# Hybrid recurrent decoder step: score products of the odd layer issued over four quarters of the array

## The chip, the cores and the metric

One core of a Trainium2 chip runs the whole program. The engines are TensorE (PE in the profile; PEld is its weight load), VectorE (DVE), ScalarE (ACT), GpSimd (POOL) and SyncE (SP). Each has its own queue, in order, and they meet at semaphores. The metric is the device time of one execution in microseconds; lower is better.

## What is computed

A trunk of two layers is run on 512 prompt tokens and on 8 sample sequences of 4 tokens. Layer 0 mixes with GLA and HGRN2, layer 1 with RWKV-7. Each layer then has a SwiGLU and a gated input embedding. Only the RWKV-7 recurrence of layer 1 matters here, 16 heads of 64:

```
def step(s, inp):
    r_t, lw_t, k_t, v_t, kk_t, a_t = inp
    s_kk = jnp.einsum('bhik,bhk->bhi', s, kk_t)
    s = (s * jnp.exp(lw_t)[:, :, None, :]
         - s_kk[..., :, None] * (kk_t * a_t)[..., None, :]
         + v_t[..., :, None] * k_t[..., None, :])
    return s, jnp.einsum('bhij,bhj->bhi', s, r_t)
```

## The kernel before, in words

The prompt is cut into 16 chunks of 32 tokens, and the recurrence is done chunk by chunk in matrix form. The sample tokens are a seventeenth chunk. The heads stand in 8 tiles i, two heads g = 0, 1 in each (partitions 0 to 63 and 64 to 127). Four chunks make a quad; quads 0 to 3 are the prompt, quad 4 is the sample. PSUM has 8 banks: banks 0 and 1 (`ps[:, bank, :]`) belong to the preparation of a quad, banks 2 to 7 to the chunks' own chain.

**Preparation of a quad** is a list of parts, made by `parts_of` (L1779). Part number k writes bank k % 2. TensorE issues the products of each part (`pe_prepare`, L1805), one named engine then takes the bank to SBUF (`act_prepare` L1860, `dve_prepare` L1886), and the next part on that bank first waits for it (`read_by`). The parts of a prompt quad, in order:

- four score parts "sc" (L1820), one for each pair of chunks cp and head half g. Each has 16 products of 64 by 64 by 64 in fp32 (8 tiles i, two chunks par). par picks the output partitions, so the column half of the array; g picks the operands' partitions, so its row half. Each leaves two matmul records. VectorE multiplies the bank by a mask (L1905). After the last it runs a chain: four copies L1915, L1920, L1923, and `next_level` (transpose L1949, mask L1950)
- two parts "vt" of value transposes (L1825), the first copied by ScalarE with four operations (L1868), the second by VectorE with four (L1928)
- for levels 2 to 5 of a triangular inversion, a P part (L1834, copied by ScalarE L1879; it needs the mask of L1950) and an X part (L1839; VectorE subtracts it in L1933 and makes the next mask), 64 products of 32 by 32 each over four diagonal tiles, with four key transposes "kt" (L1829, copied by ScalarE L1876) between them.

That makes 18 parts. The last two preparations also hold four state parts "st" each (L1845), which transpose states that a DMA on the GpSimd queue has brought (L2075, `pool_states`); the load for b + 2 is issued after st b. Quad 4 has one chunk pair, one chunk of it, two score parts, level 2 only, and a last part "rts" with 128 small products (256 records, L1854).

**The chunks** of a quad (`pe_chunk`, L1958) are a chain: products av (L1969), products with the state R (L1986), output products with the state (L1994), slot of two parts, U (L2001), slot of one part, state products H (L2011), output products o (L2016), slot of two parts. Before U, ScalarE and VectorE copy R (L2027, L2046), before H they copy U (L2031, L2051), and VectorE updates the state after H (L2060, L2064). In the slots `go_on` takes the next parts of the preparation of quad q + 1 on each of the three engines, at the same place in each queue. So the chunks of a quad offer 20 slots. What is left of the list stands behind the last chunk (`all_quads`). The preparation of quad 0 has nothing beside it.

```
            go_on(preparation, 2)
            pe.wait_ge(*O2.act.at(f"R{n}"))
            pe.wait_ge(*O2.dve.at(f"R{n}"))
```

Of the kernel before, what the change touches and what calls it, by code (L numbers as in the profile page):

```python
# [18 lines left out]
ALU = mybir.AluOpType  # L19
# [4 lines left out]
KT = D // P  # L24
# [104 lines left out]
def trunk(nc, a, o, known, seen, stop=99):  # L129
    ctx = ExitStack()  # L130
    with ctx:
# [31 lines left out]
        ps = ctx.enter_context(nc.psum_tensor("ps", [P, 8, 512], F32))  # L163
# [62 lines left out]
        for name in order:  # L226
            used[name] = tuple(ab)
            n, units = stages[name]
# [1117 lines left out]
        O2 = Section("odd_quads")  # L1346
# [3 lines left out]
        kb = mix[:, 0:8704].rearrange("p (i n s t) -> p i n s t", i=KT, n=NCO, s=2)  # L1350
# [386 lines left out]
        QUADS = TP // P  # L1737
# [35 lines left out]
        read_by = {}  # L1773
# [5 lines left out]
        def parts_of(q):  # L1779

            ncp = quad_shape(q)[2]
            parts = [("sc", (cp, g), "dve") for cp in range(ncp) for g in range(2)]
            parts += [("vt", 0, "act"), ("vt", 1, "dve")]
# [13 lines left out]
        def part_name(q, kind, x):  # L1797
            return {"sc": lambda: f"sc{q}{x[0]}{x[1]}", "st": lambda: f"st{x}", "rts": lambda: "rts"}.get(
                kind, lambda: f"{kind}{q}{x}")()

        def taken(by, q, kind, x):

            return (O2.act if by == "act" else O2.dve).at(part_name(q, kind, x))

        def pe_prepare(pe, q):  # L1805
# [5 lines left out]
            for kind, x, by, bank in parts_of(q):  # L1811
                if bank in read_by:
                    pe.wait_ge(*read_by[bank]())
                out = ps[:, bank, :]
                if kind == "sc":
                    cp, g = x
                    for i in range(KT):
                        for par in range(min(2, len(js))):
                            n = 4 * q + 2 * cp + par
                            mm = pe.matmul(out[64 * par:64 * par + 64, i * 64:(i + 1) * 64],  # L1820
                                           kb[64 * g:64 * g + 64, i, n, :, :], qr[64 * g:64 * g + 64, i, n, :, :],
                                           start=True, stop=True)
# [34 lines left out]
                read_by[bank] = lambda by=by, q=q, kind=kind, x=x: taken(by, q, kind, x)  # L1857
# [28 lines left out]
        def dve_prepare(dve, q):  # L1886
# [13 lines left out]
            for kind, x, by, bank in parts_of(q):  # L1900
                if by == "dve":
                    name = part_name(q, kind, x)
                    dve.wait_ge(*O2.pe.at(name))
                    if kind == "sc":
                        dve.tensor_tensor(scs[q % 2][0:pr, x[0], x[1], :, :],  # L1905
                                          ps[0:pr, bank, :].rearrange("p (i t) -> p i t", i=KT),
                                          scm[0:pr, q // QUADS, :].unsqueeze(1).to_broadcast([pr, KT, 64]),
                                          ALU.mult).then_inc(*O2.dve.done(name))
                        if x == (ncp - 1, 1):
# [507 lines left out]
```

## Time and profile before

| | us |
|---|---|
| median of 3 runs | 2425.63 |
| lowest and highest | 2424.89, 2429.2 |
| profiled execution | 2422.3 |
| its span, first to last instruction | 2420.5 |
| TensorE busy | 2082.6 (86%) |
| VectorE busy | 1023.9 (42%) |
| ScalarE busy | 743.4 (31%) |
| GpSimd busy | 145.3 (6%) |

The profile is of one execution, so durations are to be held against its own time of 2422.3 us. The stage of the change lies between 1373 and 1718 us of the span. A row of the timeline gives start, duration, engine, line, operation, output and input tiles, shapes and how many instructions it merges; in brackets stands the idle time of the engine before it and what ended it. "issue" is idle time for which the profile shows nothing waited for. PEclk is the clock that TensorE was granted, as a share of 2.4 GHz.

### The profile page before, as it was taken

To read this page: it belongs to the slowest core of one execution; us is meant where nothing else is said; L and a number is where in the kernel's file an instruction comes from. 1 tells how busy PE (TensorE), PEld (TensorE's weight loads), DVE (VectorE), ACT (ScalarE), POOL (GpSimd) and SP (SyncE) were. 2 spreads that over 40 slices of the span, in tenths; PEclk is the share of its full clock that TensorE was granted. 3 is DMA by queue.
4 is the path that set the end of the run, shared out by engine and by line. 5 is a ranking of instruction groups with operands and counts; after the bars stand their busy time and mean duration, and the time that the engine had idled before them with its cause. 6 is when DMAs were issued, how large, how long until landed. Compare 5 with 4: busy or idle time off the path is not lost.

```text
span 2420.5 us, 48144 instructions
## 1 busy us (share of the span) xinstructions
PE 2082.6 (86%) x21161; PEld 1931.0 (80%) x21161; DVE 1023.9 (42%) x1401; ACT 743.4 (31%) x932; POOL 145.3 (6%) x159
## 2 busy tenths in 40 slices
PE   4997658978899999986898889889768799999987
PEld 4897547848799999984787778778447799999976
DVE  5326583134433333355578533332434433333353
ACT  3125221043443222232355111121054444122233
POOL 1000352110100000010000000000010100000010
PEclk8998655558899999998899865655567899999988
DMA  3232002011223223221121200000020223222311
GB/s 102 64 90 57 27 1 53 7 52 56 93 87 101 65 87 100 74 61 46 40 74 54 62 4 3 4 12 19 11 40 27 88 87 100 74 79 87 100 48 54
DMA packets 237101, 138.59 MB, mean 57 GB/s; under 512 B 6560, under 2 KB 232160, under 8 KB 236944
## 3 DMA queue, kind: packets, MB, share of 16 engines
q1 hardware_dynamic: 226528, 114.31, 16.4%
q0 software_dynamic: 4048, 13.67, 2.3%
q10 hardware_dynamic: 6368, 8.22, 1.1%
q8 instruction: 135, 2.21, 0.4%
q14 instruction: 22, 0.18, 0.0%
HBM read 128.02 MB, written 8.16 MB: 56 GB/s over the span
## 4 chain that ended last, share of the span: by engine, by line
PE 75%; DVE 14%; ACT 5%; issue 3%; POOL 1%; DMA 1%; ACTq 0%; DVEq 0%; POOLq 0%
PE ps L299 51%; DVE mix L496 1%; DVE x_split L516 1%; PE ps L1839 1%; PE ps L1820 1%; PE ps L1969 1%; PE ps L1986 1%; PE ps L945 1%; PE ps L1994 1%; PE ps L2011 1%; PE ps L916 1%; PE ps L906 1%; PE ps L1834 1%; PE ps L2016 1%; PE ps L2001 1%
## 5 line engine op out<-in xcount | busy, mean ns | idle before, releaser
L299 PE MATMUL ps<-x_split,w_head 128*128 128x272 f32 x5568 | 952.1, 294 | 82.6 <-DVE x_split L516 39.7
L299 PEld LDWEIGHTS ps<-x_split,w_head 128*128 128x128 f32 x5568 | 807.5, 193 | 105.0 <-issue 80.3
L299 PE MATMUL ps<-x_split,w_rest 128*128 128x272 f32 x2784 | 586.4, 293 | 0.0
L267 ACT ACTIVATE w_head<-w_raw 128x1024 fp32r<-128x1024 f32 (+1 forms) x206 | 228.8, 1111 | 799.4 <-PE ps L299 791.8
L272 DVE TENSOR_TENSOR w_rest<-w_raw,w_head 128x1024 fp32r<-128x1024 f32 (+1 forms) x206 | 265.2, 1288 | 430.5 <-ACT w_head L267 430.3
L299 PEld LDWEIGHTS ps<-x_split,w_rest 128*128 128x128 f32 x2784 | 445.5, 193 | 0.0
L299 PE MATMUL ps<-hidden_split,w_head 128*128 128x272 f32 x1408 | 233.1, 287 | 0.0
L299 PEld LDWEIGHTS ps<-hidden_split,w_head 128*128 128x128 f32 x1408 | 198.0, 188 | 0.0
L299 PE MATMUL ps<-hidden_split,w_rest 128*128 128x272 f32 x704 | 145.2, 287 | 0.0
L1125 DVE TENSOR_TENSOR hT<-hT,ps 128x544 f32 (+1 forms) x48 | 34.6, 722 | 208.2 <-PE ps L299 208.2
L299 PEld LDWEIGHTS ps<-hidden_split,w_rest 128*128 128x128 f32 x704 | 110.0, 188 | 0.0
L496 POOL TENSOR_TENSOR mix<-hT,mix 128x544 f32<-128x544 f32 x20 | 36.8, 1842 | 1097.9 <-ACT mix L480 1077.6
L866 PE MATMUL ps<-mix 64*64 64x64 f32 (+1 forms) x896 | 57.8, 314 | 47.8 <-DVE mix L774 30.4
L866 PEld LDWEIGHTS ps<-mix 64*64 64x64 f32 (+1 forms) x896 | 49.7, 217 | 53.8 <-DVE mix L774 35.4
L1241 DVE TENSOR_TENSOR mix<-mix,ps 128x544 f32<-128x544 f32 x44 | 31.8, 722 | 132.2 <-PE ps L299 132.2
L267 ACT ACT_TABLE_LOAD x21 | 26.9, 1283 | 94.5 <-PE ps L299 83.8
L843 ACT ACTIVATE mix<-mix 128x512 f32<-128x512 f32 (+1 forms) x36 | 23.0, 640 | 81.6 <-POOL mix L747 81.5
L1834 PE MATMUL ps<-odd_quad 32*32 32x32 f32 x2080 | 30.3, 228 | 18.3 <-DVE odd_quad L1950 15.2
L1834 PEld LDWEIGHTS ps<-odd_quad 32*32 32x32 f32 x2080 | 28.2, 142 | 22.3 <-issue 18.3
L746 POOL TENSOR_TENSOR mix<-mix 128x256 f32<-128x256 f32 (+1 forms) x36 | 25.9, 720 | 261.0 <-DVE mix L701 197.6
L496 DVE TENSOR_TENSOR mix<-hT,mix 128x544 f32<-128x544 f32 x20 | 30.1, 1525 | 26.0 <-ACT mix L480 25.7
L466 DVE TENSOR_TENSOR mix<-mix 128x544 f32<-128x544 f32 x48 | 34.6, 720 | 11.2 <-ACT mix L460 11.2
(353 smaller groups left out, 2459.1 us busy)
## 6 DMA issues: line engine op xcount, KB each, us to landing
w_raw<-in_w_ffn_gate SPq DMA_DIRECT2D x44, 512.0 KB, 3.9
w_raw<-in_w_ffn_up SPq DMA_DIRECT2D x44, 512.0 KB, 3.8
w_raw<-in_w_ffn_down SPq DMA_DIRECT2D x32, 704.0 KB, 4.4
w_raw<-in_w_in_even SPq DMA_DIRECT2D x29, 512.0 KB, 3.8
w_raw<-in_w_ple_gate SPq DMA_DIRECT2D x16, 512.0 KB, 3.6
w_raw<-in_w_out_even SPq DMA_DIRECT2D x8, 512.0 KB, 3.7
w_raw<-in_rw_wr SPq DMA_DIRECT2D x8, 512.0 KB, 3.6
w_raw<-in_rw_wk SPq DMA_DIRECT2D x8, 512.0 KB, 3.7
```

The source lines that it names most:

```text
L267: act.activation(wh[:, s, 0:kt * P], raw[:, s, 0:kt * P], ACT.Copy).then_inc(head_ok[s], 1)
L272: dve.tensor_tensor(wl[:, s, 0:kt * P], raw[:, s, 0:kt * P], wh[:, s, 0:kt * P].bitcast(F32), ALU.subtract).then_inc(rest_ok[s], 1)
L299: mm = pe.matmul(ps[:, 2 * s + h, 0:TH], w[:, s, k * P:(k + 1) * P], x[:, k, h * TH:(h + 1) * TH], start=first and k == 0, stop=k == kt - ...
L466: dve.tensor_tensor(n.sum, n.sum, n.sq[:, s, :], ALU.add).then_inc(sum_ok, 1)
L496: eng.tensor_tensor(n.y[:, k % 3, :], hT[:, k, :], n.rs, ALU.mult).then_inc(*signal.done(f"y{k}"))
L516: dve.scalar_tensor_tensor(out=xl[:, k, :], in0=n.y[:, k % 3, :], scalar=n.gain(k), in1=xh[:, k, :].bitcast(F32), op0=ALU.mult, op1=ALU.su ...
L746: pool.tensor_tensor(e[:, :, 0, :], mid, b[:, :, 0, :], ALU.subtract)
L866: mm = pe.matmul(ps[64 * (c % 2):64 * (c % 2) + CE, b0 + level // 2, at:at + CE], left[:, c * CE:(c + 1) * CE], right[:, c * CE:(c + 1) * CE],
L906: mm = pe.matmul(ps[:, b0, h * CE:(h + 1) * CE], vtok[r:r + CE, tt, h * DV:(h + 1) * DV], pT[r:r + CE, h, tt, :], start=h == 0, stop=c == ...
L1125: dve.tensor_tensor(h, h, out2(s), ALU.add).then_inc(bank_free[s], 1)
L1241: dve.tensor_tensor(two(prod), two(act_out), out2(1), ALU.mult).then_inc(prod_ok, 1)
L1834: mm = pe.matmul(at_block(out, tile, cp, i), at_block(bT, tile, cp, i), at_block(xx, tile, cp, i), start=True, stop=True)
```

## The change

`parts_of` now lists one score part for each chunk pair, and the value transposes stand between and behind them: sc 0, vt 0, sc 1, vt 1 (with one chunk pair: sc 0, vt 0, vt 1). A score part writes both banks, head half g into bank g, and waits until both are free. Its products run over i, then par, then g, so four neighbours take the four quarters of the array. VectorE multiplies the two banks one after the other, and both banks count as taken when the second is done. A prompt quad has 16 parts in place of 18, the sample's one less. The products, their sizes and their number stay the same.

```
--- before.py
+++ after.py
@@ -1779,8 +1779,10 @@
         def parts_of(q):
 
             ncp = quad_shape(q)[2]
-            parts = [("sc", (cp, g), "dve") for cp in range(ncp) for g in range(2)]
-            parts += [("vt", 0, "act"), ("vt", 1, "dve")]
+            parts = [("sc", 0, "dve"), ("vt", 0, "act")]
+            if ncp > 1:
+                parts += [("sc", 1, "dve")]
+            parts += [("vt", 1, "dve")]
             keys = [("kt", j, "act") for j in range(2 * ncp)]
             for level in range(2, level_count(q) + 1):
                 parts.append(("P", level, "act"))
@@ -1795,7 +1797,7 @@
             return [(kind, x, by, k % 2) for k, (kind, x, by) in enumerate(parts)]
 
         def part_name(q, kind, x):
-            return {"sc": lambda: f"sc{q}{x[0]}{x[1]}", "st": lambda: f"st{x}", "rts": lambda: "rts"}.get(
+            return {"sc": lambda: f"sc{q}{x}1", "st": lambda: f"st{x}", "rts": lambda: "rts"}.get(
                 kind, lambda: f"{kind}{q}{x}")()
 
         def taken(by, q, kind, x):
@@ -1809,17 +1811,19 @@
                     pe.wait_ge(bank_free[s], used["rw_o"][s])
                 pe.wait_ge(*O1.dve.at("nrm"))
             for kind, x, by, bank in parts_of(q):
-                if bank in read_by:
-                    pe.wait_ge(*read_by[bank]())
+                banks = (0, 1) if kind == "sc" else (bank,)
+                for b in banks:
+                    if b in read_by:
+                        pe.wait_ge(*read_by[b]())
                 out = ps[:, bank, :]
                 if kind == "sc":
-                    cp, g = x
                     for i in range(KT):
                         for par in range(min(2, len(js))):
-                            n = 4 * q + 2 * cp + par
-                            mm = pe.matmul(out[64 * par:64 * par + 64, i * 64:(i + 1) * 64],
-                                           kb[64 * g:64 * g + 64, i, n, :, :], qr[64 * g:64 * g + 64, i, n, :, :],
-                                           start=True, stop=True)
+                            n = 4 * q + 2 * x + par
+                            for g in range(2):
+                                mm = pe.matmul(ps[64 * par:64 * par + 64, g, i * 64:(i + 1) * 64],
+                                               kb[64 * g:64 * g + 64, i, n, :, :], qr[64 * g:64 * g + 64, i, n, :, :],
+                                               start=True, stop=True)
                 elif kind == "vt":
                     for i in range(4):
                         mm = pe.transpose(out[0:nt, i * P:(i + 1) * P], vF[:, 4 * x + i, q * P:q * P + nt], ident[:, :])
@@ -1854,7 +1858,8 @@
                                 mm = pe.matmul(o2[:, :, b * ST:(b + 1) * ST], hs[r, i, b, :],
                                                qr[r, i, NCO - 1, :, b * ST:(b + 1) * ST], start=True, stop=True)
                 mm.then_inc(*O2.pe.done(part_name(q, kind, x)))
-                read_by[bank] = lambda by=by, q=q, kind=kind, x=x: taken(by, q, kind, x)
+                for b in banks:
+                    read_by[b] = lambda by=by, q=q, kind=kind, x=x: taken(by, q, kind, x)
                 yield
 
         def act_prepare(act, q):
@@ -1902,11 +1907,12 @@
                     name = part_name(q, kind, x)
                     dve.wait_ge(*O2.pe.at(name))
                     if kind == "sc":
-                        dve.tensor_tensor(scs[q % 2][0:pr, x[0], x[1], :, :],
-                                          ps[0:pr, bank, :].rearrange("p (i t) -> p i t", i=KT),
-                                          scm[0:pr, q // QUADS, :].unsqueeze(1).to_broadcast([pr, KT, 64]),
-                                          ALU.mult).then_inc(*O2.dve.done(name))
-                        if x == (ncp - 1, 1):
+                        for g in range(2):
+                            dve.tensor_tensor(scs[q % 2][0:pr, x, g, :, :],
+                                              ps[0:pr, g, :].rearrange("p (i t) -> p i t", i=KT),
+                                              scm[0:pr, q // QUADS, :].unsqueeze(1).to_broadcast([pr, KT, 64]),
+                                              ALU.mult).then_inc(*O2.dve.done(f"sc{q}{x}{g}"))
+                        if x == ncp - 1:
                             dve.wait_ge(*O2.dve.at(name))
 
                             for par in range(min(2, len(js))):
```

## Rows read from the trace of the kernel before

**Rows 1.** The page, busy time of TensorE and its share of the span.
```profile
PE 2082.6 (86%) x21161; PEld 1931.0 (80%) x21161; DVE 1023.9 (42%) x1401; ACT 743.4 (31%) x932; POOL 145.3 (6%) x159
```

**Rows 2.** Windows of the stage: length, busy us, PEclk, DMA share, GB/s.
```profile
1373.59:1413.39 39.80, 26.13 (x1177) 23.29 (x1178) 16.83 (x29) 7.12 (x12) 0.00 (x0) 0.59 0.05 10
1413.39:1483.44 70.05, 62.97 (x1880) 58.17 (x1880) 26.72 (x41) 13.02 (x23) 0.00 (x0) 0.57 0.02 4
1483.44:1554.51 71.07, 62.06 (x1946) 57.46 (x1944) 27.42 (x42) 13.35 (x24) 0.00 (x0) 0.64 0.01 3
1554.51:1635.52 81.01, 69.84 (x1977) 64.34 (x1977) 28.11 (x43) 14.98 (x27) 2.46 (x3) 0.56 0.04 10
1635.52:1717.50 81.98, 78.35 (x1328) 72.61 (x1328) 21.06 (x34) 10.77 (x20) 3.54 (x5) 0.50 0.09 22
```

**Rows 3.** TensorE's waits, 1373 to 1718: total us, times, longest us.
```profile
PE ps L1834 <- DVE odd_quad L1950: 15.2, 7, 3.5
PE ps L1839 <- issue: 9.3, 11, 1.9
PE ps L1845 <- DMA mix<-in_state_rwkv: 4.3, 2, 3.9
```

**Rows 4.** Timeline, TensorE: start, us, engine line, tile, shapes, records [idle before].
```profile
1373.59 6.15 PE L1820 MATMUL ps<-mix 64*64 64x64 f32 x128 [3.06 <-DVE mix L1716]
...
1448.87 1.92 PE L1994 MATMUL ps<-mix 64*64 64x32 f32 x32
...
1450.71 1.93 PE L1834 MATMUL ps<-odd_quad 32*32 32x32 f32 x128
...
1641.17 3.28 PE L1820 MATMUL ps<-mix 64*64 64x64 f32 x32
```

**Rows 5.** Chain of work, first chunk of quad 1, 1489 to 1502.
```profile
1489.28 3.11 PE ps L1820 x61
...
1501.91 1.09 PE ps L1969 x17
```

**Rows 6.** Timeline of quad 2's preparation, VectorE and ScalarE, 1501 to 1506.
```profile
1501.64 1.72 DVE L1915 COPY odd_quad<-odd_quad 32x512 f32<-32x512 f32 x4
...
1501.94 2.43 ACT L1868 ACTIVATE odd_quad<-ps 32x512 f32<-32x512 f32 x4 [2.02 <-PE ps L1825]
1503.39 0.69 DVE L1920 TENSOR_TENSOR odd_quad<-odd_quad,tables 128x512 f32<-128x512 f32 x1
...
1504.84 0.71 DVE L1949 STREAM_TRANSPOSE odd_quad<-odd_quad 128x512 f32<-128x512 f32 x1
1505.48 0.65 DVE L1950 TENSOR_TENSOR odd_quad<-odd_quad,tables 128x512 f32<-128x512 f32 x1
```

**Rows 7.** Chain of work, a chunk with an empty slot, 1702 to 1704.
```profile
1702.94 0.71 DVE mix L2051
...
1703.78 1.97 PE ps L2011 x32
```

**Rows 8.** Timeline, TensorE, quad 3 and the sample's preparation, 1633 to 1678.
```profile
1633.11 1.08 PE L1845 MATMUL ps<-ident,mix 64*128 64x64 f32 x8 [3.94 <-DMA mix<-in_state_rwkv]
...
1648.33 1.97 PE L2011 MATMUL ps<-mix 64*64 64x64 f32 x32 [1.07 <-DVE mix L2051]
...
1678.01 13.71 PE L1854 MATMUL ps<-mix 64*64 64x8 f32 x253
```

**Rows 9.** Timeline, VectorE, last mask multiply of quad 0, 1379.8.
```profile
1379.78 0.69 DVE L1905 TENSOR_TENSOR odd_quad<-ps,tables 128x512 f32<-128x512 f32 x1 [0.66 <-PE ps L1820]
```

**Rows 10.** Windows, columns as in rows 2: two stretches at either clock.
```profile
1488.00:1504.00 16.00, 15.84 (x288) 14.89 (x287) 7.28 (x13) 3.02 (x7) 0.00 (x0) 0.50 0.01 2
1511.50:1525.20 13.70, 10.70 (x461) 9.46 (x459) 4.83 (x8) 3.70 (x7) 0.00 (x0) 1.00 0.02 5
```

**Rows 11.** Timeline, TensorE: a fifth level, and L1994 at the upper clock.
```profile
1474.16 1.87 PE L1834 MATMUL ps<-odd_quad 32*32 32x32 f32 x123 [2.22 <-DVE odd_quad L1950]
...
1519.79 1.12 PE L1994 MATMUL ps<-mix 64*64 64x32 f32 x32
```

## Prediction

> **What bounds the kernel now.** I read the page first: TensorE is busy for 2082.6 us, 86% of the span [rows 1]. The change works in one stage only, the recurrence of the odd layer, from 1373.6 to 1717.5 us. The table of windows [rows 2] shows its parts: the preparation of quad 0 alone (39.8 us), quads 0, 1 and 2 (70.0, 71.1 and 81.0 us, each with the preparation of the next quad threaded through it) and quad 3 with the sample chunk (82.0 us). In all but the first TensorE is busy 86 to 96% of the time, VectorE a quarter to two fifths, ScalarE less. So TensorE's queue sets the end, and what counts is its work plus the moments at which the next instruction in it must wait. Those waits are listed in [rows 3]. The largest are VectorE's masks before the products of L1834 (15.2 us, half of it in the preparation of quad 0, and 2.2 us before each fifth level, as [rows 11]), 4.3 us for the sample states' DMA, and stretches of "issue", where no wait is shown (9.3 us in the largest row).
>
> TensorE's clock was at its lower level (1.2 GHz) for most of the stage: means of 0.50 to 0.64 [rows 2]. I sum at that level.
>
> **What a score product costs.** One fp32 product is two matmul records. In the old order neighbours lie in the same row half of the array and in its two column halves. 128 records took 6.15 us, 48 ns each [rows 4]; in the quads 61 took 3.11 us, 51 ns each [rows 5], so a part of 32 costs 1.6 us. For the sample there is only one chunk, so all products of a part take the same quarter: 32 records in 3.28 us, about 100 ns each. So two column halves run at once and a quarter that repeats does not [rows 4]. Nothing in this trace uses four quarters of 64 by 64. The nearest rows bound it. L1834 cycles over four 32 by 32 tiles that differ in rows and columns: 128 records in 1.9 us, 15 ns each against 32 columns twice, so four at once do run. L1994 takes two diagonal quarters: 32 records in some 1.85 us before L1834 follows, 58 ns, two at once over the row halves [rows 4]. By the first the new order takes half of the old time, about 27 ns a record, 1.75 us for a pair of parts (64 records) instead of 3.2; by the second alone it would not gain, 3.25 us. I take the first, since rows and columns each split in the trace and the 15 ns row shows that the queue can feed four. What neither shows is two row halves writing the same partitions, in two banks.
>
> The Trainium skill (TensorE: Matmul & The Clock Gate, Part 3, packing small matmuls) gives sixteen tiles of rows and columns at once a measured 10.6 times, with row tiles in different banks. By that page four quarters run at once; no run here shows it yet. TensorEngine Tiling (Array Packing), PSUM Bottleneck, of the Trainium skill speaks against the change: once tiling has sped up the products, emptying PSUM may be the bound.
>
> **The change on TensorE's queue.** Before, four score parts alternate between banks 0 and 1, so the products of one run while VectorE multiplies the other by the mask. After, one part fills both banks, VectorE needs two operations of 0.69 us for it, and the next part on TensorE waits for the second of them. Queued behind that wait is everything on TensorE, the chunk's own chain too. The number of parts falls from 18 to 16 for a prompt quad, so each later part also moves to an earlier slot (two, one and two slots in each chunk).
>
> 1. *First chunk of quads 0, 1 and 2*, worked out on quad 1 [rows 5, 6]. Before, from the end of the products with the state at 1489.28 to the next chunk at 1501.91, TensorE has no gap over 0.3 us. After: scores 1.75; wait for both multiplies, 2 x 0.69 and two hand-overs of 0.1, 1.6; value transposes 1.0; U products 1.85; then the second scores, whose bank 1 is free only when ScalarE has copied the values (four copies, 2.43, begun after the transposes), 0.8 of waiting; scores 1.75; state and output products 3.35; value transposes 1.0; then P of level 2, now in this chunk, which needs VectorE's two multiplies (1.4) and the chain behind them, 1.72 for the four copies, twice 0.69, 0.71 and 0.65, together 4.5. That is 6.1 us after the scores' end with hand-overs, of which 4.4 are filled, so 1.7 of waiting. VectorE's state update H now stands behind this chain too; it is wanted only after the next chunk's first products and ends in time. Waits 1.6 + 0.8 + 1.7 = 4.1; saved on scores 6.4 - 3.5 = 2.9. Net +1.2 a quad, three times: +3.6. Nothing else on TensorE changes in amount: the transposes, P and X products are the same and are only earlier.
> 2. *Last chunk of quads 0 and 1.* Two parts fewer means that the slot between U and H is empty, where X of level 5 stood. A late chunk of quad 3 shows the price of an empty slot: VectorE's copy of U from 1702.94, TensorE on again at 1703.78, 0.9 us with the hand-over [rows 7]. Two times: +1.8. The wait of 2.2 us before level 5 stays, in another slot.
> 3. *Quad 2 to quad 3.* Before, two of four state parts were left over and stood behind the chunks; the third waited for a DMA that is issued only once the first is through, 4.3 us idle with the fourth's [rows 3, 8]. After, 16 + 4 parts fill the 20 slots: the first stands before U, the third after H and the outputs, some 6 us later, more than the 3.9 that TensorE waited there with next to nothing between. -4.3. Issuing on the GpSimd queue is the same.
> 4. *Preparation of quad 0*, nothing beside it. Before, the last multiply ended at 1380.47, 6.9 us after the first product [rows 9]. After: 1.75, two multiplies 1.6, transposes 1.0, the four copies 2.5, scores 1.85, two multiplies 1.5: 10.2. The copies now stand between the two score parts. The chain behind is the same: +3.3.
> 5. *Quad 3 and the sample chunk.* The sample's scores fall from 3.2 to 1.65 (two row halves), with a wait of 1.6 for VectorE behind them; the idle 1.1 before L2011, where VectorE was late [rows 8], goes, since its queue is ahead by then (-1.0). The part with the 256 small products (L1854, 13.7 us) moves to a slot directly behind the last state part and waits 0.9 for its copy, and leaves an empty slot, 0.9 [rows 7, 8]. Together -1.6 + 1.6 - 1.0 + 0.9 + 0.9 = +0.8.
>
> VectorE and ScalarE do the same operations as before, so nothing else is added. Sum: 3.6 + 1.8 - 4.3 + 3.3 + 0.8 = +5.2 us. The profiled execution took 2422.3 us with its span of 2420.5, which gives 2427.5; the median of the runs is 3.3 us above that execution, and I add the change to the median: 2425.6 + 5.2 = 2430.8 us.
>
> What this leaves out are the "issue" gaps and the clock. In dense 32 by 32 products TensorE stops, for up to 1.9 us, with nothing shown that it waits for [rows 3], and now and then the clock rose, as from 1511.5 to 1525.2, in which 32 records of L1994 take 1.12 instead of 1.92 us [rows 4, 10, 11]. The old stage shows both, roughly in balance. After, there are more real waits beside which issue gaps can hide, and one chunk (the third) is denser. I take no net change, and 5 us to either side for the range.
>
> **Rivals.** *A: four quarters don't run at once.* Two row halves writing the same partitions might take turns. For: no row shows it. Against: the 15 ns row. Then each of the eight prompt pairs keeps 3.25 us instead of 1.75 (12.0) and the sample 3.2 instead of 1.65 (1.6), with the waits behind them unchanged: +5.2 + 13.6 = about +19, 2444 us. The products would stand in the order that the change says and not run four at once.
>
> *B: the clock makes it not slower.* Four quarters at work might hold the upper level (2.4 GHz) in the first chunk of a quad, where in quad 1 it was at the lower throughout [rows 10]. Price: in a stretch half as long as that of 13.7 us in [rows 10] such a row falls from 1.92 to 1.12, so with waits that stay about 3 us are won, in each of three quads, -9: 2422 us. It decides from two such stretches on, where the +5.2 is gone. For: the clock did rise, at 1511.5, with P of level 2 and the transposes gapless ahead of it [rows 10]. Against: behind each 1.75 us of scores there is now an idle 1.6, which is the reverse of gapless. If the first-chunk waits are also shorter than in my sum it ends near 2417.
>
> *C: instruction supply.* The "issue" gaps follow the dense products, and the scores at 27 ns are now dense as well and P of level 2 follows them; in the third chunk of a quad four level products (512 records) instead of three stand beside the chunk's own 192, about 32 ns a record without waits. One more gap of 1.8 us in each of three quads, and one in the start: +5.2 + 7 = +12, 2438 us.
>
> **How the numbers follow.** Forecast (0 to +10) 0.52, A (+15 to +25) 0.18, B (-9 to +1) 0.20, C (+10 to +15) 0.10. A measurement of this kernel can tell 0.2%, 4.9 us, from no change. The forecast's centre is just over that bound: 0.28 of it slower, 0.24 same. A and C are slower. B is half faster, half same. Faster 0.10, same 0.34, slower 0.56. The range goes from within B, 2420, to just past A's centre, 2446, and leaves out under 0.2; the forecast's own range is 2426 to 2436.
>
> **What would show it.** Score records: 64 in about 1.75 us, four starting close together; 3.2 would be A. VectorE's two multiplies in a row behind each and TensorE idle 1.6 us before the value transposes, with VectorE as the releaser. Two gaps more in each first chunk, 0.8 for ScalarE's copies and 1.7 for VectorE's masks. No 4 us wait for the state DMA before L1845. The start of quad 0's first chunk about 3.3 us later, quads 0 and 1 about 2.1 us longer each, quad 2 about 3 us shorter. The prediction is wrong if the stage's clock differs from 0.50 to 0.64, if the issue gaps change by more than 5 us, or if time moves outside of 1373 to 1718.

## The result, and the profile after

The changed kernel takes 2437.98 us (median of 12 runs, 2431.84 to 2443.83), the kernel before in the same comparison 2425.68 us (2423.55 to 2429.26). The ratio is 1.0051, interval 1.0041 to 1.006: slower, by 12.3 us. The forecast was 2430.8 us with a sum of +5.2. The sign held, and so did the wide range, 2420 to 2446. The forecast's own range, 2426 to 2436 (0.52), was missed by 2 us, and the size was less than half of what came: the number fell in rival C's band, +10 to +15, which had 0.10.

The profiled execution of after took 2436.38 us against 2422.3, so 14.1 more. First the page, busy time by engine, to be held against [rows 1]:

```profile
span 2434.6 us, 48152 instructions
PE 2075.4 (85%) x21161; PEld 1921.6 (79%) x21161; DVE 1022.5 (42%) x1401; ACT 742.4 (30%) x932; POOL 145.2 (6%) x159
```

TensorE has the same number of matmul records as before and is busy 7.2 us less, while the span is 14.1 us longer: what was added is idle time. The score products alone take 13.2 us less, so the other products take more; that is taken up below. The windows of after answer [rows 2] (window, its length, then busy time of TensorE, weight load, VectorE, ScalarE and GpSimd with their instructions, granted clock, DMA share, GB/s). They are the preparation of quad 0, quads 0, 1, 2, and quad 3 with the sample chunk.

```profile
1374.76:1418.58 43.82, 24.28 (x1176) 20.96 (x1177) 16.66 (x29) 7.11 (x12) 0.00 (x0) 0.58 0.04 9
1418.58:1492.45 73.87, 64.02 (x1882) 58.86 (x1884) 26.44 (x41) 12.98 (x23) 0.00 (x0) 0.52 0.01 3
1492.45:1566.55 74.10, 61.51 (x1947) 56.36 (x1947) 27.13 (x42) 13.36 (x24) 0.00 (x0) 0.62 0.01 3
1566.55:1647.35 80.80, 66.08 (x1979) 60.07 (x1979) 27.82 (x43) 14.94 (x27) 2.20 (x3) 0.61 0.04 10
1647.35:1731.90 84.55, 78.83 (x1329) 72.71 (x1330) 20.97 (x34) 10.75 (x20) 3.80 (x6) 0.50 0.08 22
```

The stage is 357.1 us long against 344.0, so +13.1. It starts 1.2 us later, behind code that the change doesn't touch, and what follows it is the same to 0.2 us. (The windows end with the last row of the recurrence; the stage is taken to the next product, 1717.60 and 1731.90.) The waits of TensorE in the stage answer [rows 3] (line, who released it, us in total, times, longest):

```profile
PE ps L1838 <- DVE odd_quad L1956: 22.3, 12, 3.5
PE ps L1829 <- DVE odd_quad L1911: 8.5, 6, 1.5
PE ps L1843 <- issue: 7.0, 7, 2.0
PE ps L1838 <- issue: 4.3, 3, 2.3
PE ps L2017 <- DVE mix L2057: 2.8, 4, 0.9
PE ps L1824 <- ACT odd_quad L1873: 2.6, 1, 2.6
```

Line 1838 is the old L1834, 1843 the old L1839, 1829 the value transposes, 1824 the scores. The wait for VectorE's chain grew from 15.2 us in 7 waits to 22.3 in 12, and 8.5 us in 6 waits are new, for VectorE's two multiplies (L1911). The row for the state DMA is gone.

### The profile page after: what moved, and what is told of

Same layout as the page of the kernel before. It is cut to its first block, busy times and chain, and to the rows that moved or that the text cites. A ratio compares the mean times of both kernels' runs of the same rounds, so it can differ in the third digit from the quotient of the medians.

```text
span 2434.6 us, 48152 instructions
## 1 busy us (share of the span) xinstructions
PE 2075.4 (85%) x21161; PEld 1921.6 (79%) x21161; DVE 1022.5 (42%) x1401; ACT 742.4 (30%) x932; POOL 145.2 (6%) x159
## 4 chain that ended last, share of the span: by engine, by line
PE 74%; DVE 15%; ACT 5%; issue 3%; POOL 1%; DMA 1%; ACTq 0%; DVEq 0%; POOLq 0%
PE ps L299 51%; PE ps L1975 1%; DVE mix L496 1%; DVE x_split L516 1%; PE ps L1843 1%; PE ps L1992 1%; PE ps L1838 1%; PE ps L945 1%; PE ps L2000 1%; PE ps L916 1%; PE ps L906 1%; PE ps L901 1%; PE ps L2017 1%; PE ps L2007 1%; PE ps L934 1%
## 5 line engine op out<-in xcount | busy, mean ns | idle before, releaser
L1838 PE MATMUL ps<-odd_quad 32*32 32x32 f32 x2080 | 30.5, 226 | 26.7 <-DVE odd_quad L1956 22.3
L1838 PEld LDWEIGHTS ps<-odd_quad 32*32 32x32 f32 x2080 | 28.2, 140 | 30.2 <-DVE odd_quad L1956 15.7
L2052 DVE COPY mix<-ps 32x512 f32<-32x512 f32 x17 | 11.7, 690 | 77.7 <-PE ps L1992 75.6
```

The costliest lines, as they stand in the source:

```text
L1838: mm = pe.matmul(at_block(out, tile, cp, i), at_block(bT, tile, cp, i), at_block(xx, tile, cp, i), start=True, stop=True)
```

## The steps, read in the first chunk of quad 1

The timeline of after (start, duration, engine, line, operation, tiles, shapes, instructions; in brackets the idle time before and its releaser) in the chunk on which the sum was worked out:

```profile
1497.90 1.90 PEld L1824 LDWEIGHTS ps<-mix 64*64 64x64 f32 x62
1500.08 1.29 DVE L1911 TENSOR_TENSOR odd_quad<-ps,tables 128x512 f32<-128x512 f32 x2 [2.97 <-PE ps L1824]
1501.42 1.12 PE L1829 MATMUL ps<-ident,mix 128*128 128x128 f32 x4 [1.43 <-DVE odd_quad L1911]
1502.58 2.42 ACT L1873 ACTIVATE odd_quad<-ps 32x512 f32<-32x512 f32 x4 [5.57 <-PE ps L1829]
1505.15 1.99 PE L1824 MATMUL ps<-mix 64*64 64x64 f32 x64 [0.76 <-DVE mix L2057]
1508.51 1.71 DVE L1921 COPY odd_quad<-odd_quad 32x512 f32<-32x512 f32 x4
1512.35 0.65 DVE L1956 TENSOR_TENSOR odd_quad<-odd_quad,tables 128x512 f32<-128x512 f32 x1
1513.15 1.87 PE L1838 MATMUL ps<-odd_quad 32*32 32x32 f32 x123 [2.77 <-DVE odd_quad L1956]
```

Each step of the sum is there, in order: 64 score records in 1.9 us, TensorE idle 1.43 while VectorE multiplies both banks (forecast 1.6), 0.76 at the second scores (forecast 0.8), and a wait for the chain of the masks. The last is 2.77 here, where the transposes ahead of it (L1829, 0.66 us in the same view) had run at the upper clock, and 1.6 in quads 0 and 2 at the lower (forecast 1.7). The row at 1505.15 names VectorE's copy of U as the releaser and not ScalarE's copies; both end within 0.1 us of each other there, so who of the two sets it isn't told by this row.

## Experiments

Times are medians, the kernel before beside each on the same chip. "Stage" is from the first score product to the end of the recurrence in the profiled execution: 344.0 us before, 357.1 after. One profile of a stage isn't the last word: pad, below, is in effect the kernel before profiled again, and its stage took 350.6. None of the kernels leaves work out.

**halves: do four quarters run at once?** The same parts, banks and waits, but the order of the products in a part is that of before.

```
-                    for i in range(KT):
-                        for par in range(min(2, len(js))):
-                            n = 4 * q + 2 * x + par
-                            for g in range(2):
+                    for g in range(2):
+                        for i in range(KT):
+                            for par in range(min(2, len(js))):
+                                n = 4 * q + 2 * x + par
```

> The changed kernel with one edit: in a score part all products of head half 0 come before those of head half 1, so that neighbours lie in one row half again, as in the kernel before. Banks, waits, slots and everything else are those of the changed kernel. My theory (four quarters do run at once, and the loss comes from waits): scores of a pair go back from 1.75 to 3.2 us, 8 pairs and the sample, so about 13.6 us slower than the changed kernel, near 2451 us; the idle times of TensorE beside the scores stay. Rival (the order of products brings nothing, two row halves take turns in any case): same time as the changed kernel, 2438.

2446.63 us against 2425.23, ratio 1.0091 [1.0075, 1.0108], and 8.7 us above the changed kernel; its stage is 370.0 us, 12.9 longer. Two first rows of the stage, of halves and then of after:

```profile
1373.37 3.16 PEld L1824 LDWEIGHTS ps<-mix 64*64 64x64 f32 x64 [1.34 <-issue]
```

```profile
1374.73 1.83 PEld L1824 LDWEIGHTS ps<-mix 64*64 64x64 f32 x64 [3.13 <-issue]
```

64 records take 3.16 us in the old order and 1.83 in the new, 49 and 29 ns each. So two row halves that write the same partitions in two banks run at once, which no row of before showed, and rival A falls. Eight parts at 1.33 us and the sample's at 1.3 (its chunk takes 19.6 us instead of 18.3) are 12.0 us, and the two measures of the difference, 8.7 and 12.9, lie on either side of that. The expected 2451 was 4 too high. The Trainium skill (TensorE: Matmul & The Clock Gate, Part 3) says that tiles of rows and columns run at once; the trace agrees, 1.83 us.

**order: is it the value transposes between the scores?** Scores of both pairs first, then both transposes.

```
-            parts = [("sc", 0, "dve"), ("vt", 0, "act")]
-            if ncp > 1:
-                parts += [("sc", 1, "dve")]
-            parts += [("vt", 1, "dve")]
+            parts = [("sc", cp, "dve") for cp in range(ncp)] + [("vt", 0, "act"), ("vt", 1, "dve")]
```

> The changed kernel with the parts in the order sc 0, sc 1, vt 0, vt 1, still 16 parts. Theory (a sum of the waits on TensorE): the 2.6 us wait for ScalarE's value copies in the preparation of quad 0 goes (about -3.7 us there), the 0.8 us waits in the three first chunks go too, but the second score part now waits directly for the two multiplies of the first, and the mask chain then holds back the U copy on VectorE: first chunks 1.4 us longer each. Sum +0.7 against the changed kernel, so no difference, 2437 to 2441. Rival (waiting for ScalarE's copies is the main cost of the new list): 6 us faster than the changed kernel, 2432.

2434.83 us, ratio 1.0037 [1.0025, 1.0049], stage 356.6. The preparation of quad 0 falls from 43.8 to 39.9, since the 2.6 us for ScalarE's copies are gone, but the first chunks of quads 1 and 2 grow from 22.4 to 24.1. The waits of TensorE in order say why:

```profile
PE ps L1835 <- DVE odd_quad L1953: 14.9, 8, 2.6
PE ps L2014 <- DVE odd_quad L2054: 10.0, 4, 3.8
PE ps L2014 <- DVE mix L2054: 7.6, 5, 3.8
PE ps L1821 <- DVE odd_quad L1908: 6.1, 4, 1.6
```

L2014 is the state product H, and L2054 VectorE's copy of U, which now stands behind VectorE's four multiplies and chain. In the stage the wait only changed its place; the median is 3.2 us under the changed kernel, 2 below the expected range. The list is in the same order on three engines, and a part that is good for TensorE's queue can be bad for VectorE's.

**slots and thin: does the shift of the later parts cost?** slots keeps the changed scores and transposes but adds two empty parts behind them, so that every later part is in its old slot. thin adds one empty part ahead of the fifth level's P, and so takes that part out of the third chunk.

```
+            none = ("none", 0, None, 0)
-                parts += [("sc", 1, "dve")]
-            parts += [("vt", 1, "dve")]
+                parts += [("sc", 1, "dve", 0), ("vt", 1, "dve", 1), none, none]
+            else:
+                parts += [("vt", 1, "dve", 0), none]
```

> The changed kernel with two empty parts behind vt 1 (one for the sample), which cost nothing and only put each later part back into the slot that it had in the kernel before. Theory (waits at the head of the list): P of level 2 no longer waits 1.6 us, the empty slot before H is filled again, but the 4.3 us wait for the states' DMA comes back; -2.6 against the changed kernel, 2435. Rival (the crowded third chunk of a quad, 708 records, runs into the supply of instructions, which would be the 6 us that my sum missed): third chunks fall from 22.5 or 23 to 17.5 to 19 us, and the time to 2429 to 2431.

2431.74 us, ratio 1.0022 [1.0011, 1.0033]: 6.2 us of the 12.3 are gone, 3.3 more than my theory had and 0.7 short of the rival's range. Its stage is 354.9; quad 0 is back at 70.2 us and quad 3 at 81.1, and the third chunks of quads 0 to 2 fell to 19.7, 15.9 and 18.5, as the rival had it, but the wait of 4.3 us for the state DMA is back too, and quad 2 takes 85.5. So its stage is only 2.2 us under after's (4.6 under that of changed_again), and 4.4 us of the gain in this profile lie behind the stage, in code that no run changes. How much of the 6.2 is the shift of the parts isn't shown.

```
+            if q < QUADS:
+                parts.insert(parts.index(("P", 5, "act")), ("none", 0, None))
+                at = len(parts) - (4 if q == 3 else 0) - 3
+                return [(kind, x, by, (k if k <= at else k - 1) % 2) for k, (kind, x, by) in enumerate(parts)]
```

> The changed kernel with one empty part ahead of P of level 5 in quads 1 to 3 (and 0, where it costs nothing), so that P of level 5 goes from the crowded third chunk into the fourth: 580 matmul records there instead of 708. By my sum of waits the third and fourth chunk together get 1.5 us shorter in quads 0 and 1 and 2 us longer in quad 2, where one state part is left over again: -0.8 us in all, 2437. Theory (the time that my sum for the change missed, some 6 us, comes from the crowded chunk): 4 to 7 us faster than the changed kernel, 2431 to 2434. Rival (it comes from elsewhere): within 2 us of it.

2440.07 us, ratio 1.0054 [1.0041, 1.0067], on a chip where the changed kernel took 2436.91 (ratio 1.004 [1.0027, 1.0054]). In quad 0 the third and fourth chunks are 19.4 and 17.3 us instead of 23.3 and 13.9: nearly the same sum. Quad 2 is 3.0 us longer, where I expected 2. The whole is 3.2 us slower than the changed kernel, where the theory wanted 4 to 7 faster. So the fault isn't that one crowded chunk; that reason of mine fell.

**changed_again: how steady is the stage?** The changed kernel once more, for its second profile.

> The changed kernel itself, beside the two that follow on the same chip. By every theory 0.5% slower than the kernel before, 2436 to 2440; its first chunks of quads 0 to 2 at 18.6 and 22.4 us, since those are sums of waits and lower-clock products, while the third chunks may differ from the first profile, where they hang on the clock and the issue gaps.

2436.91 us. Its stage is 359.5, with 43.8, 74.1, 76.1, 80.8 and 84.8 for the parts. Quad 2 is the point of interest; its window in changed_again:

```profile
1569.30:1650.10 80.80, 68.82 (x1980) 62.80 (x1980) 27.82 (x43) 14.92 (x27) 2.32 (x3) 0.56 0.04 10
```

The same 80.80 us as in after, where the mean clock was 0.61. In after some 7 us more were at the upper clock, and TensorE was busy 2.7 us less, but it stood 7.2 us in "issue" instead of 4.8. The faster clock was given back in such stops.

**states: what is the DMA wait worth alone?** The kernel before, with the first two state parts of the last prompt quad moved up into its list, so that the load of the third is issued early.

```
-            if q >= 3:
+            if q == 3:
+                parts[10:10] = [("st", 0, "act"), ("st", 1, "dve")]
+                parts += [("st", 2, "act"), ("st", 3, "dve")]
+            elif q > 3:
```

> The kernel before with state parts 0 and 1 moved up in the list of quad 3, behind the second key transposes, so that the loads of states 2 and 3 land before their parts come. Nothing else changes. Theory: the 4.3 us idle of TensorE between quads 2 and 3 goes, as it did in the changed kernel; 2421 to 2423. Rival (that time is given back as a longer chain elsewhere, in which case my -4.3 in the sum was wrong): 2425 to 2427.

2419.09 us, ratio 0.9969 [0.9954, 0.9985], -5.7 us, and quad 2 takes 75.5 us instead of 81.0. That is 2 us below the expected range. The term of -4.3 was right, if anything small.

**spread: can the new order be had without its waits?** Quad 0: both score parts, then both transposes. The other prompt quads: each score part in the last slot of a run, an empty slot behind it, so that the chunk's own products stand on TensorE while VectorE multiplies; bank 0 is given free after the first multiply. spread_halves is spread with the old order of products, spread_states is spread with the edit of states.

```
+            if q == 0:
+                parts = [("sc", 0, "dve", 0), ("sc", 1, "dve", 0), ("vt", 0, "act", 0), ("vt", 1, "dve", 1)]
+            elif ncp > 1:
+                parts = [("sc", 0, "dve", 0), none, ("vt", 0, "act", 0), ("sc", 1, "dve", 0), none,
+                         ("vt", 1, "dve", 1)]
...
+                if kind == "sc":
+                    read_by[0] = lambda q=q, x=x: O2.dve.at(f"sc{q}{x}0")
```

> Four quarters as in the changed kernel, but the list made so that nothing on TensorE waits behind a score part: for quads 1 to 3 sc 0, empty, vt 0, sc 1, empty, vt 1, then the rest in the slots of the kernel before; for quad 0 sc 0, sc 1, vt 0, vt 1; bank 0 counts as free after the first multiply. Theory: the gain on the products (1.5 us a pair) is all that is left, first chunks 15.5 us in place of 18.5, sample 1.6 less, the preparation of quad 0 about equal; -10 us against the kernel before, 2415. Rival (TensorE's time goes to instruction supply or clock instead, whatever the waits): within 4 us of the kernel before, 2422 to 2430.

> The list of the run spread with the products of each score part in the old order, head half 0 first. Theory (four quarters carry all of the gain): 13.6 us more of score products, so 3 us slower than the kernel before, 2427 to 2430, since one part for both banks has slightly longer waits than the four parts of before. Rival (the new list itself is what gains): within 4 us of the run spread, 2412 to 2420.

> The run spread with state parts 0 and 1 moved up in the same way. Theory: the two gains add, -10 and -4: 2411 to 2413. Rival (they don't add, since quad 2 is held by the supply of instructions): 2415 to 2417.

| | this | before beside it | ratio | stage |
|---|---|---|---|---|
| spread | 2416.03 | 2425.23 | 0.9953 [0.994, 0.9967] | 340.5 |
| spread_halves | 2426.94 | 2424.8 | 1.0002 [0.9989, 1.0015] | 349.3 |
| spread_states | 2405.94 | 2424.8 | 0.9912 [0.9893, 0.9932] | 332.1 |

spread beats the kernel before by 9.2 us, as expected, and the changed one by 22. It differs from spread_halves in the order of the products alone, and that order is worth 10.9 us between them (8.8 in the stage; the two ran on different chips). spread_halves is as fast as the kernel before: the new list alone gains nothing. The stage of spread is 3.5 us under that of before and 10.0 under pad's; the gain of 9.2 goes by the medians. The first chunk of quad 0 in spread, TensorE alone:

```profile
1414.38 1.92 PE L1986 MATMUL ps<-odd_quad 32*32 32x64 f32 x32 [0.83 <-issue]
1416.23 1.98 PE L1833 MATMUL ps<-mix 64*64 64x64 f32 x64
1418.14 1.92 PE L2018 MATMUL ps<-mix,odd_quad 32*32 32x64 f32 x32
1419.99 1.11 PE L1838 MATMUL ps<-ident,mix 128*128 128x128 f32 x4
1421.03 1.97 PE L2028 MATMUL ps<-odd_quad,mix 64*64 64x64 f32 x32
```

Behind the scores (L1833) stand the chunk's own U products (L2018), for which nothing has to be waited. There is no gap, and the first chunks are 12.0, 15.7 and 15.7 us against 14.6, 18.4 and 18.4 before. With the state parts moved up as well the gains of the two add at least: 5.7 + 9.2 = 14.9 against 18.9 measured, 5 us below the expected 2411. The intervals of the three ratios allow a plain sum.

**pad and padw2: is it instruction supply?** In the kernel before, instructions that do nothing, ahead of each product of the chunks. In pad they are idle ones, in padw2 two waits for values that were reached long ago, 1584 instructions in all.

```
+                    pe.wait_ge(*O1.dve.at("nrm")); pe.wait_ge(*O1.act.at("rs"))
```

> The kernel before with one idle instruction of no length ahead of each product of the chunks' own chain (96 in a chunk, some 1600 in all, the size of 6.4 fetches of 256 instructions). These products follow each other every 116 ns at the lower clock, so an extra instruction can be taken beside them. Theory (the gaps called issue are TensorE waiting for the next block of instructions, which come no faster than one in 3.6 us): first chunks of a quad, where there is room, change by under 0.5 us each, and the dense second to fourth chunks of quads 0 to 2 get longer by 1 to 2 us each, 10 to 20 us in all, 2435 to 2445. Rival (the gaps have another cause, so only what TensorE does counts): under 4 us, 2422 to 2429. If the first chunks grow as much as the dense ones, the idle instruction has a cost of its own and the run tells nothing about the supply.

> The kernel before with two waits that have long been met ahead of each product of the chunks' own chain, of which one becomes an instruction of its own: 1584 more on TensorE, 6.2 blocks of 256; the earlier run of this kind brought none of its idle instructions into the program. These products follow each other every 116 ns at the lower clock. Theory (the gaps called issue are TensorE waiting for its next block): first chunks of a quad unchanged within 0.5 us, the dense second to fourth chunks 1 to 2 us longer each: 10 to 20 us in all, 2435 to 2445, with six more fetches in the stage. Rival (the gaps have another cause): under 4 us. If the first chunks grow as much as the dense ones, the wait has a cost of its own and only the difference between them counts for the supply.

pad took 2427.15 us, ratio 1.0011 [0.9996, 1.0025]. The program had 48164 instructions instead of 48144 and the same number of fetches: the idle instructions weren't in it, so it says nothing of the supply. But it is a second profile of the kernel before, and its stage took 350.6 us (40.0, 70.1, 73.6, 84.4 and 82.5 for the parts) instead of 344.0. padw2 took 2471.29, ratio 1.0179 [1.0164, 1.0193], with 71 fetches in the stage instead of 65 and a stage of 390.6 us, far more than the 10 to 20 us expected. It doesn't decide either. The first chunks grew too, from 14.6, 18.4 and 18.4 us to 15.5, 20.0 and 19.9, so the added waits cost something of themselves (32 records of L1988, the old L1986, took 2.50 us instead of 1.92), and only 14 us of the stage were at the upper clock instead of 48. Three causes moved at once.

## Why the forecast was right in sign and short in size

| | sum | after less before | changed_again less pad |
|---|---|---|---|
| preparation of quad 0 | +3.3 | +4.0 | +3.8 |
| quad 0 | +2.1 | +3.8 | +4.1 |
| quad 1 | +2.1 | +3.0 | +2.5 |
| quad 2 | -3.1 | -0.2 | -3.6 |
| quad 3 and sample | +0.8 | +2.5 | +2.2 |
| stage | +5.2 | +13.1 | +9.0 |

The third column holds the second profiles of the same two kernels against each other. The medians say +12.3 for the whole. Where the two columns agree the term is firm; quad 2 differs by 3.4 us between them.

**What held.** Step 1, the first chunks: 18.6, 22.4 and 22.4 us after, 14.6, 18.4 and 18.4 before. The sum is +1.2, and +2.9 for the P and the transposes that now stand in that chunk: +4.1 against +4.0 measured, three times. The weighing of the two bounds for the four quarters, and the price of the empty slot (0.9, as [rows 7]), held too. The Trainium skill (TensorEngine Tiling (Array Packing), PSUM Bottleneck) says that with tiling the emptying of PSUM may become the bound. The trace agrees: 1.4 to 1.5 us idle behind a score part for the two multiplies.

Step 4, the preparation, has the forecast steps: the last multiply ends 10.5 us after the first product, for 10.2. Another 0.4 is in stops and seams behind it.

**Which term failed.** The whole stage in before, pad, after and changed_again, columns as in [rows 2]:

```profile
1373.59:1717.60 344.01, 299.45 (x8305) 275.97 (x8306) 120.14 (x189) 59.24 (x106) 6.00 (x8) 0.57 0.04 10
1372.06:1722.62 350.56, 303.37 (x8305) 279.35 (x8306) 120.12 (x189) 59.13 (x106) 5.98 (x8) 0.56 0.04 10
1374.76:1731.90 357.14, 294.72 (x8304) 268.96 (x8306) 119.00 (x189) 59.13 (x106) 6.00 (x8) 0.56 0.04 10
1375.30:1734.81 359.51, 300.75 (x8305) 274.97 (x8306) 119.04 (x189) 59.10 (x106) 6.01 (x8) 0.54 0.04 10
```

| TensorE in the stage, us | sum | before | pad | after | changed_again |
|---|---|---|---|---|---|
| waits with a releaser on another engine or a DMA | about +18 | 28.6 | 28.5 | 47.3 | 47.0 |
| stops called issue | 0 | 16.5 | 17.3 | 15.5 | 12.2 |
| busy with score products | about -13 | 31.6 | 31.6 | 18.4 | 18.4 |
| busy with everything else | 0 | 267.9 | 271.8 | 276.3 | 282.4 |

The +18 are three times 4.1 and twice 0.9, less 4.3, with about 6 in step 4 and 2.4 in step 5. The -13 are three times 2.9, some 2.7 in step 4 and 1.6 in step 5.

The waits of the sum came, 18.7 us of them, and so did the saving on the scores, 13.2. What the sum had at nothing is the last row. "Nothing else on TensorE changes in amount: the transposes, P and X products are the same and are only earlier" was the wrong step. The number of records is the same, but they took 8.4 us more (10.6 between the second profiles).

A part of that is the clock, for which the prediction said "I take no net change". Over the stretches at the upper level TensorE was busy for 34.0 us in before and for 30.8 in after (29.2 in pad, 20.5 in changed_again). By the price of 1.92 us at the lower level for 1.12 at the upper [rows 4, 11] that is 2.3 us between before and after, and 6.2 between the second profiles. Two profiles of one kernel bear the price out roughly: pad was busy at the upper level for 4.8 us less than before, which it puts at 3.4, and the last row is 3.9 longer; for changed_again and after it is 10.3 us, priced at 7.4, and 6.0. The rest of the last row, some 4 to 6 us, is dearer neighbours, of which the next paragraphs show about half.

**Where the 7.9 us are, part by part, between before and after.**

*Step 5, quad 3 and the sample, +1.7.* No clock and no issue stop is in the way here, so it can be read row by row. Right were: scores with their wait, 3.4 us instead of 3.2; the idle 1.07 before H gone; the wait 0.88 before L1858; one empty slot. Not in the sum: the state parts, four in each of the last two preparations. Two of them in one slot took 1.60 us before, and take more when they stand apart. First before, then after:

```profile
1667.35 1.60 PE L1845 MATMUL ps<-ident,mix 64*128 64x64 f32 x16
```

```profile
1675.22 1.11 PE L1849 MATMUL ps<-ident,mix 64*128 64x64 f32 x8
1679.82 1.92 PE L1849 MATMUL ps<-ident,mix 64*128 64x64 f32 x16
1687.43 1.11 PE L1849 MATMUL ps<-ident,mix 64*128 64x64 f32 x8
```

That is 4.0 us to the starts of what follows instead of 3.05, +0.9. The pair in one slot is also dearer, 1.92, and why I can't say. The rest, +0.8, is at seams: before, the records of the sample's two small level parts and of L1854 mixed with those of the next products and overlapped; after, they stand beside other neighbours and don't (0.3, 0.3 and 0.15 us). So "only earlier" isn't free: what a part costs depends on its neighbours.

*Step 3, quad 2, +2.9.* The DMA wait went as forecast. Against it stand the state parts again (about +0.9), a wait of 0.6 for VectorE before level 3, and stops. The issue stops of quad 2 are 4.0 us before, 7.2 in after. The third chunk holds most of them (quad 2's chunks in before, then in after, columns as above):

```profile
1554.51:1572.90 18.39, 18.23 (x325) 17.11 (x324) 5.71 (x9) 1.95 (x4) 0.00 (x0) 0.50 0.01 3
1572.90:1590.79 17.89, 17.73 (x461) 15.99 (x461) 10.54 (x18) 5.12 (x9) 0.00 (x0) 0.50 0.01 3
1590.79:1608.19 17.40, 15.02 (x584) 13.71 (x584) 5.73 (x9) 3.96 (x7) 0.00 (x0) 0.73 0.02 4
1608.19:1635.52 27.33, 18.86 (x629) 17.53 (x622) 6.13 (x9) 3.96 (x7) 2.46 (x3) 0.54 0.10 22
```

```profile
1566.52:1588.91 22.39, 18.42 (x454) 16.87 (x456) 10.04 (x17) 4.29 (x8) 0.00 (x0) 0.50 0.01 2
1588.91:1607.05 18.14, 16.60 (x483) 14.90 (x471) 6.93 (x11) 3.95 (x7) 0.00 (x0) 0.59 0.01 4
1607.05:1629.58 22.53, 13.70 (x705) 12.33 (x708) 6.69 (x10) 3.35 (x6) 0.00 (x0) 0.80 0.02 4
1629.58:1647.32 17.74, 17.36 (x376) 15.97 (x366) 4.15 (x6) 3.35 (x6) 2.17 (x3) 0.50 0.12 33
```

The third chunk had a clock of 0.80 and TensorE was busy for 13.7 us of it, yet it took 22.5. In quad 0 of after the chunk with the same work took 23.1 at 0.57. So some 13.6 us at the upper level instead of 3.4 bought half a microsecond: TensorE was busy 4.7 us less, and its stops grew by 3.6. Of the 8.8 us idle, 2.2 and 0.6 are waits for VectorE and 5.9 are stops.

*Quads 0 and 1, +1.7 and +0.9.* Quad 0's second chunk was at a clock of 0.70 before; after, all of quad 0 but one chunk was at 0.50. That is 10.2 us at the upper level before (16.9 x 0.4 and 19.2 x 0.18) and 3.4 after. At the price above the 6.8 us are worth up to 4.9. Against that its stops fell from 4.8 to 3.1. In quad 1 the stops fell from 5.9 to 3.1, the waits before levels 2 and 3 are 1.1 and 0.6 more than in the sum, and 3.4 us less are at the upper clock, up to 2.4. Both come to within 1.5 us of what was measured. But quad 1 took 73.6 us in pad, 2.6 more than in before, and quad 2 84.4, 3.4 more, with nothing changed: the terms of single quads are no firmer than that.

So two things were put at nothing: the price of the other products, by "only earlier", and the exchange of clock and stops, by "I take no net change". The stops of the whole stage didn't grow, 16.5 us before and 15.5 after, and the stage's clock stayed inside of the bounds that I named. But they moved, out of quads 0 and 1, where real waits cover them, into quad 2, and less of TensorE's work fell in the time at the upper level. About 2.6 us of dearer neighbours (the state parts twice, and the seams of step 5) are shown in rows. The rest, some 5 us, is an account from two profiles each, of which the clock's share is 2.3 us in one pair and 6.2 in the other. I know no run that holds clock and stops still, so the split of these 5 us stays open.

**The rivals.** A fell by halves. B, the clock, was wrong: the mean of quad 0 fell from 0.57 to 0.52, and where it rose most, in quad 2 (0.56 to 0.61), the part took 80.8 us, as it did in changed_again at 0.56, so nothing was won. C gave the measured time, 2438, but by luck: it priced four more stops, and the stops of the stage didn't grow.

## What to carry to other kernels

Packing products over all quarters of the array pays only if something else stands on TensorE's queue while the filled banks are emptied; here an order of products that is worth 9 to 11 us came with a loss of 12.3 in the first list and with a gain of 9.2 in a list that was made for it. When a list of parts moves by a slot, look at each part beside its new neighbours on every queue, and look for what the new place lets start earlier: one DMA issued in time was worth 5.7 us. A sum of waits can be right to a microsecond and the forecast still be short: compare, too, what the untouched products cost in their new place. Where stops without a releaser and a varying clock make up some per cent of a stage, don't put their exchange at zero because each looks small alone, and take a second profile of the same kernel before you explain 3 us in one quad of one.

## What the runs showed of the hardware

- Four 64 by 64 quarters run at once in fp32 even where two row halves write the same partitions in two banks: 29 ns a record at the lower clock, against 49 for two at once and about 100 for one (3.28 us for 32).
- Stops without a releaser follow the instruction fetches. In after's third chunk of quad 2 the DMA view shows five fetches of 16 KB on the instruction queue, in 40 slices of 0.56 us:

```profile
GB/s 0 0 0 0 0 29 0 0 0 0 0 29 0 0 0 0 0 29 0 0 0 0 0 0 29 0 0 0 0 0 0 0 0 0 0 29 0 0 0 0
q8 instruction: 5, 0.08, 1.5%
```

By their packets they start at 1609.97, 1613.43, 1617.12, 1620.60 and 1626.90. TensorE's five stops there, of 0.74, 0.29, 1.08, 2.01 and 1.75 us, end at 1612.30, 1615.98, 1619.29, 1623.19 and 1629.31:

```profile
1623.19 0.58 PE L1843 MATMUL ps<-mix,odd_quad 32*32 32x32 f32 x25 [2.01 <-issue]
1629.31 0.49 PE L1838 MATMUL ps<-odd_quad 32*32 32x32 f32 x21 [1.75 <-issue]
```

Each is 2.2 to 2.6 us after its fetch began. In the stage 14 of after's 15 stops and 16 of before's 17 end 2.1 to 2.7 us behind the start of a fetch. The 16611 matmul and weight-load records of before's stage came in 65 such fetches, 256 a fetch, and no two fetches are closer than 3.2 us in the stage of any run here (the expectation of pad had 3.6). That would explain why a faster clock won nothing in a dense chunk: its 1413 records are five and a half fetches, by these numbers an estimate of some 18 us, whatever the clock. That the fetch causes the stop is argued from this order and not shown by a run: the idle instructions of pad weren't in the program, and padw2 moved the clock as well.
- A wait that was long met isn't free on TensorE: with two of them ahead of each product, each stretch of 32 records of L1988 took 2.3 to 2.6 us instead of 1.92 at the lower clock (padw2).
